# Differential attention in a two-layer trunk: maps turned three blocks behind the scores, rotation inside the input projection, outputs split per head

## What is computed

```python
def _diff_attn(q, k, v, lam):
    ...
        s = jnp.einsum("bqhmd,bnhmd->bhmqn", qi, k2).astype(jnp.float32) * scale
        p = jax.nn.softmax(s, axis=-1)
        amap = p[:, :, 0] - lam * p[:, :, 1]
        return jnp.einsum("bhqn,bnhe->bqhe", amap.astype(v.dtype), v)
...
    q, k, v = jnp.split(h @ W["w_in_c"][j], 3, axis=-1)
...
        keys = jnp.concatenate([k_ctx, _rope_pairs(k, rope)], axis=1)
        vals = jnp.concatenate([v_ctx, v], axis=1)
        o = _diff_attn(_rope_pairs(q, rope), keys, vals, lam)
    of = o.astype(jnp.float32)
    of = of * lax.rsqrt(jnp.mean(of * of, axis=-1, keepdims=True) + SUBLN_EPS) * W["c_subln"][j] * (1.0 - lam_init)
    out = of.astype(h.dtype).reshape(bn, t, C_HEADS * C_VDIM) @ W["w_out_c"][j]
```

## Time and profile before

| | us |
|---|---|
| runs (each the time of one execution) | 3380.32, 5007.38, 3377.43 |
| median of the runs | 3380.32 |
| the profiled execution | 3366.71 |
| its span on the core | 3364.9 |
| its mean granted clock of PE | 0.923 |

### The profile page before, as it was taken

One profiled execution on the slowest core, in us unless ns is written; L12 is line 12 of the kernel. 1 busy time (PEld: TensorE's weight loads), 2 busy tenths in 40 slices (PEclk: granted clock), 3 DMA queues, 4 the chain that ended last, 5 costly groups with the idle time before them and its releaser, 6 DMA issues.

```text
span 3364.9 us, 65428 instructions
## 1 busy us (share of the span) xinstructions
PE 3076.0 (91%) x28476; PEld 2905.8 (86%) x28476; DVE 1610.6 (48%) x2436; ACT 964.0 (29%) x1626; POOL 0.2 (0%) x4
## 2 busy tenths in 40 slices
PE   7799999996678887999999999999998787999998
PEld 7799999995567676999999999999995457999998
DVE  2455555654355654546465555555314554432324
ACT  1221212322344332321212322212324553322222
POOL 0000000000000000000000000000000000000000
PEclk6799999996779988999999999999997778999998
DMA  6344444210000002244444344434221011222221
GB/s 206 84 129 122 116 133 115 69 39 2 1 18 6 6 4 52 70 113 138 112 138 122 91 125 120 127 111 122 66 68 39 14 32 56 70 75 75 75 75 57
DMA packets 393617, 268.89 MB, mean 80 GB/s; under 512 B 12203, under 2 KB 372934, under 8 KB 393286
## 3 DMA queue, kind: packets, MB, share of 16 engines
q1 hardware_dynamic: 393414, 265.90, 28.3%
HBM read 257.61 MB, written 4.06 MB: 78 GB/s over the span
## 4 chain that ended last, share of the span: by engine, by line
PE 86%; DVE 8%; ACT 3%; issue 2%; DMA 1%; SPq 0%; DVEq 0%; ACTq 0%
PE banks L2421 65%; PE banks L1650 2%; PE banks L2445 2%; PE banks L2376 2%; PE banks L1690 1%; PE banks L843 1%; PE banks L435 1%; PE banks L410 1%; PE banks L826 1%; DVE big L2224 1%; PE banks L837 1%; PE banks L2452 1%; PE banks L420 1%; DVE h_lo_as_f L1423 1%; PE banks L1682 1%
## 5 line engine op out<-in xcount | busy, mean ns | idle before, releaser
L2421 PE MATMUL banks<-h_hi,w_hi 128*128 128x320 f32 x3600 | 822.8, 310 | 20.6 <-DVE w_lo L2123 20.1
L2421 PE MATMUL banks<-h_lo,w_hi 128*128 128x320 f32 x3600 | 821.2, 309 | 0.0
L2421 PE MATMUL banks<-h_hi,w_lo 128*128 128x320 f32 x3600 | 821.0, 309 | 0.0
L2421 PEld LDWEIGHTS banks<-h_hi,w_hi 128*128 128x128 f32 x3600 | 602.6, 188 | 22.1 <-issue 20.9
L2421 PEld LDWEIGHTS banks<-h_lo,w_hi 128*128 128x128 f32 x3600 | 603.3, 188 | 0.0
L2421 PEld LDWEIGHTS banks<-h_hi,w_lo 128*128 128x128 f32 x3600 | 602.6, 188 | 0.0
L2421 PE MATMUL banks<-big_as_f32r,w_hi 128*128 128x320 f32 x2816 | 529.9, 310 | 5.5 <-DVE w_lo L2123 4.3
L2123 DVE TENSOR_TENSOR w_lo<-raw,w_hi 128x1024 fp32r<-128x1024 f32 x333 | 399.2, 1219 | 224.0 <-ACT w_hi L2007 223.2
L2007 ACT ACTIVATE w_hi<-raw 128x1024 fp32r<-128x1024 f32 x333 | 341.6, 1050 | 447.5 <-DMA raw<-ffn_w 292.5
L2421 PEld LDWEIGHTS banks<-big_as_f32r,w_hi 128*128 128x128 f32 x2816 | 442.7, 188 | 6.6 <-DVE w_lo L2123 5.1
L2268 DVE TENSOR_TENSOR work<-work,banks 128x640 f32<-128x640 f32 x88 | 72.2, 821 | 604.9 <-PE banks L2421 591.2
(11 more groups left out here) (349 smaller groups left out, 2803.9 us busy)
## 6 DMA issues: line engine op xcount, KB each, us to landing
raw<-ffn_w SPq DMA_DIRECT2D x272, 512.0 KB, 5.1
work<-mod_w SPq DMA_DIRECT2D x136, 512.0 KB, 3.8
raw<-w_in_c SPq DMA_DIRECT2D x24, 512.0 KB, 3.7
raw<-w_in_ab SPq DMA_DIRECT2D x21, 512.0 KB, 4.0
w_hi_as_f<-mod_w SPq DMA_DIRECT2D x8, 512.0 KB, 4.5
raw<-w_out_ab SPq DMA_DIRECT2D x8, 512.0 KB, 4.9
work<-big SPq DMA_DIRECT2D x64, 64.0 KB, 2.3
raw<-w_out_c SPq DMA_DIRECT2D x8, 512.0 KB, 5.1
```

The lines of the kernel that those rows point to most:

```text
L2421: ins = nc.tensor.matmul(ps[:, c, 0:HALF], w, v[:, k, c * HALF:(c + 1) * HALF], start=(k == 0 and w is hi and v is xh), stop=(k == kts - 1 ...
```

## The change

- Latency in the pipeline: PE turns the map of block g-3 instead of g-2 (`LAG = 3`), and DVE makes the difference of block g-2.
- `turn_map` makes four transposes ahead of the scores of block g; `turn_last` makes the fifth behind the 384-column scores, which now stand directly behind the 512-column ones. ACT copies the map in two pieces (512 and 128 columns), and the values wait for both.
- The takes of the heads stand inside steps 0, 1 and 2 of the loop (`TAKE_AT`).
- The scale goes into the copy of the queries in the input projection, and the maxima are written negated, so that L1837 has no counterpart.
- The block's output row is scaled on DVE (`out_rows`) into the place of the head's queries; ACT only squares it.
- Square roots are made for the head pairs (0,1), (2,3), (4,5) and for 6 and 7. At the steps of `OUT_AT` (13, 21, 29) PE turns the outputs of two heads; ACT copies them into the high halves of the output projection's input and DVE writes the low halves (`low`). The splits after the stage are gone, and those of the first two slabs of the output weights stand at its end.
- The rotation of head h is made by DVE in iteration 10 + h of the input projection, behind the split of a slab, and SP issues its DMAs in iteration 15 + h of its own list (which runs ahead by the ring). The rotated keys are written in place; ACT copies head 0's and seven DMAs of 256 KB copy the others.

```diff
+        CSTEPS = NB * CH
+        LAG = 3
...
+        TAKES = {0: (0, 2, 4, 6), 1: (1, 3, 5, 7)}
+        TAKE_AT = {0: (0, 1, 2), 1: (3, 4, 5), 2: (6, 7)}
...
+        ROOTS = [(0, 1), (2, 3), (4, 5), (6,), (7,)]
+        OUT_AT = {NB * hs[-1] + 9: hs for hs in ROOTS[0:3]}
...
+            if j == 5:
+                for i, name in enumerate(("c_lq1", "c_lq2", "c_lk1", "c_lk2")):
+                    sp.dma_start(c_lq[:, i, :], T[name].to_broadcast([P, HD])).then_inc(c_lam, 16)
+            if j == 6:
+                sp.dma_start(c_kpast, T["cache_c_k"][0, 0]).then_inc(c_load, 16)
+            if j == 7:
+                sp.dma_start(c_vpast, T["cache_c_v"][0, 0]).then_inc(c_loadv, 16)
+            h = j - 15
+            if 0 <= h < CH:
                 sp.wait_ge(pair_free, IN_C + CH + h + 1 + RING)
                 if h > 1:
                     sp.wait_ge(CDR.s, CDR.value("k", h - 2))
                 for g in range(8):
                     o = (g ^ 1) * 16
                     sp.dma_start(c_rt[h % 2][g * 16:g * 16 + 16, :, :], big[o:o + 16, h:h + CH + 1:CH, 0:LAT]).then_inc(c_rot[h % 2], 16)
...
+        def sp_attn_c(sp):
+            sp.wait_ge(CDR.s, CDR.value("k", CH - 1))
+            sp.wait_ge(pair_free, IN_C + C_TILES + RING)
+            for h in range(1, CH):
+                sp.dma_start(c_keys[h][:, P:TOK], big[:, h + CH, 0:LAT]).then_inc(c_keyd, 16)
...
+                    if h == 0:
+                        pe.wait_ge(c_key0, 1)
+                    elif h == 1:
+                        pe.wait_ge(c_keyd, 16 * (CH - 1))
+                    taken(pe, h)
...
+                part(h, b, 1, 0, 384).then_inc(CPS.sem(f"x{b}"), 1)
 
             def scores_rest(h, b):
-                part(h, b, 1, 0, 384).then_inc(CPS.sem(f"x{b}"), 1)
...
+                if h == 0 and b == 0:
+                    taken(pe, 7)
+                for c in range(4):
+                    ins = tp(C_TURN[:, c * P:(c + 1) * P], c_a[b % 2][:, c * P:(c + 1) * P], ident)
...
+            def turn_last(h, b):
...
+                    h2, b2 = divmod(NB * h + b - 1, NB)
+                    pe.wait_ge(CDO.s, CDO.value(f"o{b2}", h2))
+                ins = tp(C_TURN4, c_a[b % 2][:, 512:640], ident)
...
+                ins.then_inc(CPT.sem(f"u{b}"), 1)
...
+                pe.wait_ge(CAT.s, CAT.value(f"u{b}", h))
...
+            for g in range(CSTEPS + LAG):
+                h, b = divmod(g, NB)
+                h3, b3 = divmod(g - LAG, NB)
+                for t in TAKE_AT.get(g, ()):
+                    turn_rows(t)
+                if g >= LAG:
+                    turn_map(h3, b3)
+                if g in OUT_AT:
+                    pe.wait_ge(CAE.s, CAE.value(f"e{(g - 2) % NB}", (g - 2) // NB))
+                    for t in OUT_AT[g]:
+                        turn_out(t)
+                    turn_last(h3, b3)
+                    values(h3, b3)
+                    pe.wait_ge(CAF.s, CAF.value("f", OUT_AT[g][-1]))
+                    pe.wait_ge(c_lo, OUT_AT[g][-1] + 1)
+                if g < CSTEPS:
                     scores_first(h, b)
-                    if b == 3 and h:
-                        turn_out(h - 1)
-                    elif h2 >= 0:
-                        turn_map(h2, b2)
+                if g >= LAG and g not in OUT_AT:
+                    turn_last(h3, b3)
+                if g < CSTEPS:
                     scores_rest(h, b)
-                    if b == 3 and h:
-                        turn_map(h2, b2)
-                    if h2 >= 0:
-                        values(h2, b2)
-            for b in (2, 3):
-                turn_map(CH - 1, b)
-                values(CH - 1, b)
+                if g >= LAG and g not in OUT_AT:
+                    values(h3, b3)
+                if g == CSTEPS + LAG - 2:
+                    turn_out(CH - 2)
             turn_out(CH - 1)
 
...
-                ins = af(c_at[b % 2].rearrange("p c n -> p (c n)"), C_TURN, ACT.Copy)
+                af(c_at[b % 2][:, 0:4, :].rearrange("p c n -> p (c n)"), C_TURN, ACT.Copy).then_inc(CAT.sem(f"t{b}"), 1)
+                act.wait_ge(CPT.s, CPT.value(f"u{b}", h))
+                ins = af(c_at[b % 2][:, 4, :], C_TURN4, ACT.Copy)
...
+                act.wait_ge(CDO.s, CDO.value(f"o{b}", h))
+                for bb in ((b,) if b < NB - 1 else (b, NB)):
+                    ins = af(c_sq[bb], c_o(h)[:, bb, :], ACT.Square, accum_out=c_ss[:, h, bb:bb + 1])
...
+            def root(hs):
+                act.wait_ge(CAO.s, CAO.value("r3", hs[-1]))
+                z = slice(hs[0], hs[-1] + 1)
...
+            af(c_keys[0][:, P:TOK], big[:, CH, 0:LAT], ACT.Copy).then_inc(c_key0, 1)
+            for g in range(CSTEPS + LAG):
...
+                if g >= LAG:
+                    turned(*divmod(g - LAG, NB))
+                for h in OUT_AT.get(g, ()):
+                    finish(h)
...
+                if g >= LAG + 1:
+                    rows(*divmod(g - LAG - 1, NB))
+                for hs in ROOTS[0:3]:
+                    if g == NB * hs[-1] + 7:
+                        root(hs)
+                if g == CSTEPS:
+                    nc.scalar.preload_act_table(ACT.Sqrt)
+                    root(ROOTS[3])
+                    split(0)
+                    split(1)
...
+            h = j - 10
+            if 0 <= h < CH:
+                dve.wait_ge(pair_free, IN_C + CH + h + 1 + RING)
+                if h:
+                    dve.wait_ge(CDR.s, CDR.value("k", h - 1))
+                v.tensor_tensor(c_t1, big[:, h:h + CH + 1:CH, 0:LAT], cos.unsqueeze(1).to_broadcast([P, 2, LAT]), ALU.mult
+                                ).then_inc(CDR.sem("c"), 1)
+                dve.wait_ge(c_rot[h % 2], 128 * (h // 2) + 128)
+                v.tensor_tensor(c_rt[h % 2], c_rt[h % 2], sin.unsqueeze(1).to_broadcast([P, 2, LAT]), ALU.mult
+                                ).then_inc(CDR.sem("s"), 1)
+                dve.wait_ge(CDR.s, CDR.value("s", h))
+                v.tensor_tensor(big[:, h, 0:LAT], c_t1[:, 0, :], c_rt[h % 2][:, 0, :], ALU.add).then_inc(CDR.sem("q"), 1)
+                v.tensor_tensor(big[:, h + CH, 0:LAT], c_t1[:, 1, :], c_rt[h % 2][:, 1, :], ALU.add).then_inc(CDR.sem("k"), 1)
...
-                ins = v.tensor_reduce(c_mx[:, h, b, :], c_scores(b), AX.X, ALU.max)
-                if last:
-                    ins = v.tensor_reduce(c_mx[:, h, NB, :], C_CTX, AX.X, ALU.max)
-                ins.then_inc(CDM.sem(f"m{b}"), 1)
-                dve.wait_ge(CDM.s, CDM.value(f"m{b}", h))
-                z = NQ if last else b + 1
-                v.tensor_scalar(c_neg[:, h, b:z, :], c_mx[:, h, b:z, :], -SCALE, None, ALU.mult).then_inc(CDM.sem(f"n{b}"), 1)
+                ins = v.tensor_reduce(c_neg[:, h, b, :], c_scores(b), AX.X, ALU.max, negate=True)
...
+            def out_rows(h, b):
+                dve.wait_ge(CPP.s, CPP.value(f"v{b}", h))
+                for bb, src in ((b, C_O), (NB, C_OP)):
+                    if bb == b or b == NB - 1:
+                        ins = v.tensor_scalar(c_o(h)[:, bb, :], src, c_rd[:, h, bb, 0:1], None, ALU.mult)
...
+                for k in hs:
+                    ins = v.tensor_tensor(c_o(k), c_o(k), c_rs[:, k, :].unsqueeze(2).to_broadcast([P, NQ, P]), ALU.mult)
...
+            def low(h):
+                dve.wait_ge(CAF.s, CAF.value("f", ROOTS[root_no(h)][-1]))
+                v.scalar_tensor_tensor(out=h_lo[:, h, :], in0=c_turn(h), scalar=csub, in1=f32(h_hi[:, h, :]),
+                                       op0=ALU.mult, op1=ALU.subtract).then_inc(c_lo, 1)
...
+            for g in range(CSTEPS + LAG):
+                for h in TAKE_AT.get(g, ()):
...
+                if g >= LAG + 1:
+                    out_rows(*divmod(g - LAG - 1, NB))
+                if 2 <= g <= CSTEPS + 1:
+                    difference(*divmod(g - 2, NB))
+                for hs in ROOTS[0:3]:
+                    if g == NB * hs[-1] + 8:
+                        scaled(hs)
+                for h in OUT_AT.get(g, ()):
+                    low(h)
+                if g < CSTEPS:
...
+                        if (kind, l % 2) == ("in", 1):
+                            sp_in_c(sp, j)
...
-                if FRESH(i):
+                if FRESH(i) and (kind, l % 2) != ("out", 1):
```

267 lines of the change are left out of this document (122 added, 145 removed).

## The result

The changed kernel takes 3277.45 us (median of 4 runs, 3273.51 to 3294.73), the kernel before 3378.88 (median of its 4 runs; the one of 5007.38 is left out of the comparison). The ratio is 0.9719, 95% interval 0.9671 to 0.9768: 2.8% faster. The forecast for the median was 3300 us.

The account below looks back on a forecast made before the run. Attention stage bound by hand-overs and a 0.77 clock, the projection by PE. 16.5 + 127.6 + 15.9 + 14 + 17 = 191.0 against 271.2 us, gain 80.2: 3286.5 profiled, 3300 median; range 3272 to 3345.

Parts of the forecast that it names:

- Step: Ordinary block step of the attention stage: 4.4 us each, 29 steps, 127.6 us; ends 3.66 and 5.4.
- Start: Blocks 0 to 2 of the attention stage, with the takes of the heads: 16.5 us, between 13 and 22.
- Pair events: Three points in the attention stage where two heads' outputs are rooted and turned: 5.3 us each, 15.9 in all.
- Low clock: Time lost to the lower clock in the attention stage: 14 us, giving clock 0.93; ends 0 and 39.
- Tail: End of the attention stage, from the last scores to the output projection: 17 us, 15 to 20.
- Input projection: Rotation moved onto DVE in the input projection before the attention stage: cost 0, bounds -2 and 18 us.
- its signs: Expected in the profile: stage about 190 us, clock over 0.9, block 4.2 to 4.6, largest PE wait 1.8 for low halves.
- waits that come back in every step (1): Rival, attention steps: 1 us per step stays open around the fifth transpose, +29 us, 3329; chance 0.17.
- stay at the lower level (3): Rival, whole attention stage at the lower clock: steps of 8.1 us, stage 290, total 3400, slower; chance 0.03.
- the projection did not pay (4): Rival, input projection: splits stand behind the rotation and PE waits up to 18 us, 3318; chance 0.05.
- The clock (2): Rival, attention stage: clock stays at 0.77, 177 us of full-clock work take 230, +39, 3339; chance 0.15.
- my two reasons: For a higher stage clock: PE has work for over 90% against 76%; low stretches begin behind PE waits such as 2.97 us.

Follow-up runs that it names:

- the run with transposes: Changed kernel plus 12 idle 128 x 128 transposes ahead of each of two PE waits in the three pair events; 3269.22 us, ratio 0.9700.
- The two runs on the end: First two output-slab splits moved later: on the changed kernel with a root per head, 3284.55 us; on that with idle transposes and reordered end, 3262.86 us.

## Why the prediction was right

The forecast was 80.2 us less in the profiled execution; it was 87.4. Term by term:

- *Step.* 4.4 forecast, 4.08 measured, 9 us less over 29. Of the 0.2 for hand-overs half is there (0.43 once in four steps), a block without a head's end takes 3.72 where I had 3.66 + 0.25, and a head's end adds 0.9 instead of 1.15. That the pipeline would be covered holds by three runs: without the third block 106.8 us come back, with the pipeline of before 40 to 64, with one piece 10.4.
- *Start.* 16.5, and 5 for the clock, forecast, 21.3 measured for the three steps. The sum agrees better than its parts: at full clock these steps take 18.2, 1.7 more than I had, and the low clock costs 3.1 in them and 1.8 behind them.
- *Pair events.* 5.3 forecast. The step takes 11.04, the next one, whose scores are all there early, 2.4 at full clock (2604.00 to 2606.41 in the run with transposes); together 13.4 against 8.2 for two ordinary ones: 5.3. That it is the forecast to the tenth is in part luck. The wait for the low halves is where it was put, 1.75 (1.8). The one for the exponentials is 1.86 and not 1.1, since two table loads stand ahead of them and I had counted one. The delays of 1.0 that I had put on DVE don't show as such; in their place PE waits 0.42 and 0.37 for the small copies. The ten transposes take 1.15 (1.4).
- *Low clock.* 14 forecast: 5 in the start and 3 for each event. 4.8 in and behind the start, 4.4 behind the first event (19.5 us from its scores to the fourth after them, 15.05 in the run with transposes), 3 behind the second, none behind the third, and 2.4 in the end, where I had none (5.6 us at a mean clock of 0.58): 14.6. The sum agrees, its parts less so.
- *Tail.* 17 forecast with bounds of 15 to 20, 20.1 measured. This is the term that was mis-sized. I gave the queue of ACT from the last scores 7.8 us and let PE wait inside it. The copy of block 30's map stood behind exponentials, a table load, the root and both slab splits; the splits ended 8.9 us after the scores, the copy 9.5. PE stood 4.54 us, and the clock fell behind that (0.58 from 2711.4 to 2717.0), which I hadn't priced. So head 6's transposes and the values of block 30 were done at 12.9 instead of 9.9, and these 3 us stay to the end. The two runs on the end have tails 3.9 and 5.4 shorter than the changed kernel's (16.2 and 14.7 from the last scores).
- *Input projection.* Nothing, as forecast: 157.2 and 157.3.

Two readings of the prediction were wrong without harm. It takes 11 of 15 table loads off ACT; 7 are left (two for each event and one at the end), so 8 are gone. And it says that its own terms reach down to 3272 with steps of 4.0 and no clock cost, which by its own numbers is 3274. Of its signs the block is outside the one it gave, on the good side (4.08 against 4.2 to 4.6), and the largest wait of PE is that of the end and not that for the low halves.

Of the rivals, waits that come back in every step (1) did not show, the stage did not stay at the lower level (3), and the projection did not pay (4). The clock (2) did not stay at 0.77 but rose to 0.90. Of my two reasons for that the first was too strong: PE has work for 84% of the stage (154.9 of 184.4), not for over 90%. The second stands as far as the runs go: low stretches follow waits of PE, and filling the waits of the events took them away each time, but such waits without a fill had a fall behind them only five times in nine. In the start the clock fell or stayed with the same instructions; what decides that is open.

The rule of the Trainium skill ("TensorE: Matmul & The Clock Gate", Part 4: PE-mode transpose) that a transpose doesn't count as busy time for the clock is not borne out: with 12 idle transposes in the place of each wait the clock stayed at 1.00, as with matmuls, and the start, where transposes lie together, ran at 1.00 from end to end in two executions. The measurement decides. In the kernel before, too, more than transposes stands ahead of the low scores that I took for the rule: two waits of PE, 1.64 and 1.65 us, lie between.

The stage was forecast at 191.0 us and took 184.4. By place the difference of 6.6 is 0.2 less in the start, 9.5 less in the 29 steps with their events, and 3.1 more in the tail. How much of the 86.8 is the clock and how much the waits can't be parted cleanly: a wait taken away changes both. The windows give the size: PE's idle time fell by 36.2 us and its busy time by 50.6, the latter by the clock and by the overlap of the 384 columns, about 13.

## What to carry to other kernels

On a pipeline of several engines, count what lies between an item's last input and the step that uses it, and put the consumer one item further back if that is longer than a step: with the order of the changed kernel this one number decides over 106.8 us, more than the whole gain. Price a wait of PE twice, once as itself and once as the slower clock that may follow it; where it can't be removed, idle transposes that are no longer than the wait are cheap cover (0.5 us per event here, against 0 to 4.4 for the fall). Before you read a few microseconds out of one profile, compare a stretch that the edit doesn't touch: here the start alone differed by 4.8. At the end of a stage, look at what stands ahead of the last copies in each queue: work that is due later belongs behind them.
